# A fused encoder layer: shorter candidate lists for one group's choices, an earlier close of its gathered tiles, and pair weights on another engine

## The chip, the core and the metric

The program runs on one core of a Trainium2 chip. The metric is the device time of one execution in microseconds (us); lower is better. The core has TensorE (PE) for matmuls, VectorE (DVE), ScalarE (ACT), GpSimd (POOL) and SyncE (SP), which here only issues DMA transfers. Each engine runs its own instructions in order and meets the others at semaphores.

## What is computed

One layer of a bidirectional encoder for two groups of rows with shared weights: prompt (1024 rows) and sample (256 rows), 1024 columns, all float32. Attention comes first, then an expert retrieval, which is where most of the time goes:

```python
def layer(x):                                   # for the prompt and for the sample
    x = x + mixer(rmsnorm(x, g_mix))            # projection, windowed and dense attention, gates, output
    x = x + peer(rmsnorm(x, g_ffn))
    return rmsnorm(x, g_final)

def peer(h):                                    # 8 heads, 2 x 128 keys, 128*128 experts
    sc = einsum(h @ w_query, sub_keys)          # rows x 8 x 2 x 128
    s_top, i_top = top_k(sc, 16)
    cand = s_top[..., 0, :, None] + s_top[..., 1, None, :]      # 16 x 16 sums
    best, pos = top_k(cand, 16)                 # and the expert numbers at pos
    g = softmax(best)
    u, v = expert_u[idx], expert_v[idx]         # 128 rows of 2 x 1024 for each row of h
    return sum_k g_k * gelu(u_k . h) * v_k
```

## The kernel before

The program is a row of phases with a barrier between two of them (the helper that ends a phase has line 91): projection, attention and merge of the sample; the sample's query phase; projection, attention and merge of the prompt; and last one long mixed phase for the prompt's experts.

**The query phase of the sample** (`phase_query`). SP loads the sample's rows `xn`, the row `gffn` of the expert norm, query weights, keys, `iota`, and the row `gmix` of the prompt's first norm. VectorE waits for both norm rows (one semaphore, `gain_ld`, 32) and for ScalarE's root, scales the rows to `h_` (L1439, L1441), PE transposes them and multiplies by the query weights of one head (`qp`, L1468) and then by its keys (`sc`, L1478). `choose(h)` on VectorE finds the best 16 of 128 keys twice, for two row tiles (`top16`, L1389 to L1397), forms the 16 x 16 sums `cand` (L1410), takes the best 16 of 256, and turns each position into its two key numbers by comparing (`hit`, L1420), multiplying (L1425) and summing (L1428). Beside it GpSimd scales one tile of the prompt's rows for each head (L1327, L1329) with `gmix` and a reciprocal that VectorE makes between two heads (`invert`, L1434); PE transposes it for the projection that comes next. With the phase's end the sample's numbers and gates are stored.

**The sample's experts** are gathered beside other work: tile 0 within the prompt's projection, tile 1 within its attention and merge (class `Hidden`, named `bg` in the phases). GpSimd fetches a row of `[u | v]` per slot with an indirect DMA; VectorE makes the dot product (L165), ScalarE the gelu (L203), VectorE the weight (L174) and the sum (L182). `Plan` spreads 128 such slots over the host phase's units. At the end `load_last` (L133, L134) loads the residual and the last norm's row into memory that the phase has finished with, `finish` and `square_root` make the normed result (L188 to L195, L208), `store` (L138) writes it. In the projection, which has 80 units of one row tile and one chunk of 512 columns, all of these come after the loops; in the merge `load_last` is issued earlier and the rest comes after the last residual (L1195).

**The mixed phase** (`phase_mixed`). Five row tiles of the prompt (`GATHERED`) are computed like the sample's, by gathered rows, but the weighted sum is made on PE: for a step of two slots VectorE makes two dots (L2244), ScalarE one gelu (L2055), two weights `wgt` (L2062) and two diagonal matrices `diag` (L2069), and PE multiplies the gathered `v` rows by them into `acc` (L2387). The ring has 8 slots; GpSimd refills two when PE's matmuls on them are done (L1963). Three tiles (`DENSE`) run over all experts, by PE (L2409, L2425), with gates built as a matrix (L2232, L2372, L2044). The choices of all eight tiles are made within the phase. The class `Turns` writes one order of all this, which every engine walks for its own part; `step(n, g)` is tile n's step g, where the dots and gelu are those of pair g and weights and matmuls those of pair g − 1.

## Time and profile before

| | |
|---|---|
| median of 3 runs | 4585.46 us (4581.51 to 4603.41) |
| the profiled execution | 4589.69 us, its span 4587.9 us |
| busy | PE 3973.8, DVE 2810.5, ACT 1275.5, POOL 1256.6 us |
| moved by DMA | 1383.03 MB, 301 GB/s over the span |
| phases: sample's query | 396 to 566 us |
| prompt's projection, attention, merge | 568 to 1142, to about 1710, to 2076 us |
| mixed phase | 2076 to 4588 us |

The profile shows one execution; its times are microseconds from the start of the span. A busy share is a mean over phases with different limits. In a row of the timeline, the idle time in brackets is that of the engine before the instruction, with what ended it. A group's "idle before" adds these up over its instructions.

### The profile page before, as it was taken

To read this page: it belongs to the slowest core of one execution; us is meant where nothing else is said; L and a number is where in the kernel's file an instruction comes from. 1 tells how busy PE (TensorE), PEld (TensorE's weight loads), DVE (VectorE), ACT (ScalarE), POOL (GpSimd) and SP (SyncE) were. 2 spreads that over 40 slices of the span, in tenths; PEclk is the share of its full clock that TensorE was granted. 3 is DMA by queue.
4 is the path that set the end of the run, shared out by engine and by line. 5 is a ranking of instruction groups with operands and counts; after the bars stand their busy time and mean duration, and the time that the engine had idled before them with its cause. 6 is when DMAs were issued, how large, how long until landed. Compare 5 with 4: busy or idle time off the path is not lost.

```text
span 4587.9 us, 61700 instructions
## 1 busy us (share of the span) xinstructions
PE 3973.8 (87%) x22629; PEld 2042.4 (45%) x22629; DVE 2810.5 (61%) x6794; ACT 1275.5 (28%) x3556; POOL 1256.6 (27%) x1018
## 2 busy tenths in 40 slices
PE   7776599998799989997993677779999899999998
PEld 3454444443577764444441344433434343344443
DVE  1332856776888876663878877645555555555544
ACT  0221111221455551112233455522121221122122
POOL 0200232221534413320232232222333222332331
PEclk9888799999899999998995789889999999999999
DMA  6243398886544348756698899999999899999997
GB/s 240 76 180 120 110 364 318 335 354 233 208 176 183 143 167 341 296 227 238 260 347 325 329 396 377 357 366 374 396 411 409 347 407 369 399 402 385 391 403 300
DMA packets 353597, 1383.03 MB, mean 301 GB/s; under 512 B 27152, under 2 KB 112784, under 8 KB 233872
## 3 DMA queue, kind: packets, MB, share of 16 engines
q0 software_dynamic: 129024, 939.58, 51.5%
q1 hardware_dynamic: 162992, 395.47, 23.1%
q10 hardware_dynamic: 61280, 44.04, 2.9%
q8 instruction: 180, 2.95, 0.3%
q14 instruction: 121, 0.99, 0.1%
HBM read 1283.52 MB, written 95.47 MB: 301 GB/s over the span
## 4 chain that ended last, share of the span: by engine, by line
PE 29%; DMA 9%; DVE 9%; issue 4%; ACT 3%; POOL 1%; ACTq 0%; SPq 0%; DVEq 0%; POOLq 0%
PE prompt_exp_wk L2425 10%; PE prompt_exp_wk L2409 10%; DMA prompt_exp_ring<-in_experts_dram,prompt_exp_idx 7%; PE prompt_exp_acc L2387 5%; PE prompt_exp_wk L2333 3%; DVE prompt_exp_junk L2244 3%; DMA gates_dram<-prompt_exp_area 2%; ACT prompt_exp_diag L2069 1%; ACT prompt_exp_wgt L2062 1%; POOL prompt_exp_ring L1963 1%; DVE prompt_exp_hit L2188 1%; DVE prompt_exp_topi L2139 1%; DVE prompt_exp_hT L2232 1%; DVE prompt_exp_top L2136 0%; PE prompt_exp_wk L2372 0%
## 5 line engine op out<-in xcount | busy, mean ns | idle before, releaser
L1963 POOL DMA_INDIRECT prompt_exp_ring<-in_experts_dram,prompt_exp_idx x640 | 698.8, 1092 | 1809.3 <-PE prompt_exp_acc L2387 1605.0
L2244 DVE CUSTOM_DVE_ANT_0 prompt_exp_junk<-prompt_exp_ring,prompt_exp_h 128x1024 bf16<-128x1024 f32 x640 | 762.0, 1222 | 239.7 <-DMA prompt_exp_ring<-in_experts_dram,prompt_exp_idx 225.9
L2425 PE MATMUL prompt_exp_wk<-prompt_exp_area 128*128 128x512 f32 x1536 | 706.2, 607 | 6.5 <-DVE prompt_exp_area L2272 6.5
L2409 PE MATMUL prompt_exp_wk<-prompt_exp_hT,prompt_exp_area 128*128 128x384 f32 x2048 | 702.7, 497 | 0.0
L2387 PE MATMUL prompt_exp_acc<-prompt_exp_ring,prompt_exp_diag 32*32 32x512 f32 x10240 | 392.5, 640 | 267.8 <-ACT prompt_exp_diag L2069 267.7
L537 PE MATMUL prompt_proj_acc<-normed_w,normed_hT 128*128 128x512 f32 x1280 | 553.6, 595 | 14.5 <-PEq L91 14.5
L2409 PEld LDWEIGHTS prompt_exp_wk<-prompt_exp_hT,prompt_exp_area 128*128 128x128 f32 x2048 | 387.3, 193 | 343.9 <-issue 111.0
L152 POOL DMA_INDIRECT sample_hid_ring<-in_experts_dram,sample_hid_idx x256 | 278.8, 1089 | 893.8 <-DVE sample_hid_acc L182 844.3
L2425 PEld LDWEIGHTS prompt_exp_wk<-prompt_exp_area 128*128 128x128 f32 x1536 | 282.2, 191 | 432.7 <-issue 385.8
L2282 DVE TENSOR_TENSOR prompt_exp_area<-prompt_exp_area,prompt_exp_wk 128x512 f32<-128x512 f32 x186 | 127.7, 687 | 519.0 <-PE prompt_exp_wk L2425 495.5
L2055 ACT ACTIVATE prompt_exp_ge<-prompt_exp_dot 128x2 f32<-128x2 f32 x320 | 65.0, 203 | 1241.6 <-DVE prompt_exp_dot L2244 1240.2
L537 PEld LDWEIGHTS prompt_proj_acc<-normed_w,normed_hT 128*128 128x128 f32 x1280 | 243.6, 191 | 318.3 <-issue 318.3
L165 DVE CUSTOM_DVE_ANT_0 sample_hid_junk<-sample_hid_ring,sample_hid_h 128x1024 bf16<-128x1024 f32 x256 | 349.6, 1365 | 42.0 <-DMA sample_hid_ring<-in_experts_dram,sample_hid_idx 31.4
L182 DVE SCALAR_TENSOR_TENSOR sample_hid_acc<-sample_hid_ring,sample_hid_w,sample_hid_acc 128x1024 f32<-128x1024 f32 x254 | 330.5, 1301 | 7.4
L2387 PEld LDWEIGHTS prompt_exp_acc<-prompt_exp_ring,prompt_exp_diag 32*32 32x32 f32 x10240 | 79.4, 105 | 467.1 <-ACT prompt_exp_diag L2069 382.1
L2069 ACT ACTIVATE prompt_exp_diag<-prompt_exp_fold,prompt_exp_wgt 128x32 f32<-128x32 f32 x640 | 170.7, 314 | 10.6 <-PE prompt_exp_acc L2387 0.2
L2372 PE MATMUL prompt_exp_wk<-prompt_exp_area,prompt_exp_hT 128*128 128x128 f32 x768 | 114.8, 308 | 41.6 <-DVE prompt_exp_hT L2232 28.2
L2062 ACT ACTIVATE prompt_exp_wgt<-prompt_exp_ge,prompt_exp_g 128x1 f32<-128x1 f32 x640 | 149.0, 280 | 0.0
L537 PE MATMUL sample_proj_acc<-sample_proj_w,sample_proj_hT 128*128 128x512 f32 x320 | 139.5, 598 | 9.3 <-PEq L271 9.3
L2232 DVE TENSOR_SCALAR prompt_exp_hT<-prompt_exp_iota,prompt_exp_ijgT 128x128 f32<-128x128 f32 x384 | 106.0, 352 | 65.8 <-PE prompt_exp_wk L2372 62.6
L2372 PEld LDWEIGHTS prompt_exp_wk<-prompt_exp_area,prompt_exp_hT 128*128 128x128 f32 x768 | 106.8, 219 | 82.4 <-DVE prompt_exp_hT L2232 56.1
L998 PE MATMUL prompt_att_Op<-prompt_att_vB,prompt_att_pT_b 128*128 128x128 f32 x1024 | 125.9, 276 | 10.4 <-ACT prompt_att_pT_a L712 10.4
(363 smaller groups left out, 4987.8 us busy)
## 6 DMA issues: line engine op xcount, KB each, us to landing
prompt_exp_area<-in_u_turned_dram SPq DMA_DIRECT2D x128, 512.0 KB, 8.4
prompt_exp_area<-in_experts_dram SPq DMA_DIRECT2D x64, 1024.0 KB, 13.3
gates_dram<-prompt_exp_area ACTq DMA_DIRECT2D x12, 2048.0 KB, 29.2
prompt_exp_area<-gates_dram SPq DMA_DIRECT2D x32, 768.0 KB, 14.6
sample_proj_w<-in_w_all_dram SPq DMA_DIRECT2D x10, 2048.0 KB, 13.9
normed_w<-in_w_all_dram SPq DMA_DIRECT2D x10, 2048.0 KB, 15.2
proj_dram<-prompt_proj_stage SPq DMA_DIRECT2D x80, 256.0 KB, 5.4
prompt_exp_ring<-in_experts_dram,prompt_exp_idx POOLq DMA_INDIRECT x640, 10.1
```

The lines of the kernel that those rows point to most:

```text
L152: self.nc.gpsimd.indirect_dma_start(out=self.ring[:, s % self.RING, :], out_offset=None, in_=self.experts, in_offset=bass.IndirectOffsetOn ...
L165: self.nc.vector.tensor_tensor_reduce(out=self.junk[:], in0=self.ring[:, s % self.RING, 0:D], in1=self.h[:], scale=1.0, scalar=0.0, op0=AL ...
L182: nc.vector.scalar_tensor_tensor(self.acc[:], v, w, self.acc[:], ALU.mult, ALU.add).then_inc(self.added, 1)
L537: last = nc.tensor.matmul(acc[:, u % 4, :], hT[:, k, t * P:(t + 1) * P], w[:, c % NL, k, :], start=(k == 0), stop=(k == KD - 1))
L1963: nc.gpsimd.indirect_dma_start(out=ring[:, s % RING, :], out_offset=None, in_=experts, in_offset=bass.IndirectOffsetOnAxis(ap=idx[:, n % 2 ...
L2062: last = nc.scalar.activation(wgt[:, s:s + 1], ge[:, s:s + 1], ACT.Copy, scale=g2[:, n % 2, s:s + 1])
L2069: last = nc.scalar.activation(diag[:, (g - 1) % 2, c, :], fold[:], ACT.Copy, scale=wgt[:, s:s + 1])
L2244: nc.vector.tensor_tensor_reduce(out=junk[:, s % 2, :], in0=ring[:, s % RING, 0:D], in1=h2[:, n % 2, :], scale=1.0, scalar=0.0, op0=ALU.mu ...
L2372: last = nc.tensor.matmul(wk[:, 2 + i % 2, c * KEYS:(c + 1) * KEYS], onehot_a[:, i % 2 * BLOCK + c, :], onehot_b[:, i % 2, c, :], start=Tr ...
L2387: last = nc.tensor.matmul(acc[at:at + Q, part, :], diag[k, (g - 1) % 2, c, :], ring[k, s % RING, D + half * 512:D + half * 512 + 512], sta ...
L2409: last = nc.tensor.matmul(wk[:, j % 2, 0:TURNED], ut[:, j % 3, k, :], hT_dense[:, k, :], start=(k == 0), stop=(k == KD - 1))
L2425: last = nc.tensor.matmul(wk[:, 2 + o % 2, :], act_e[:, c % 2, j, t * P:(t + 1) * P], vt[:, half, j, :], start=(j == 0), stop=(j == JB - 1))
```

## The change

1. In `phase_query`, `choose(h)` forms 80 of the 256 sums for each row tile: all 16 with the best first key, 7 x 8 for the next seven, and 8 with the best second key (only these can be among the best 16). The position in this list is turned into two key numbers by five small operations on float32 and compared, in bf16, with two rows of a `table`. Comparing takes two instructions of 512 elements, multiplying one of 1024.
2. `gmix` gets a semaphore of its own, `mix_ld`, which GpSimd waits for; VectorE waits for `gffn` alone.
3. In `phase_project`, the plan of the gathered tile ends at unit 77 (`UNITS - 3`). SP issues `load_last` at unit 74; `square_root` and `finish` are made at unit 77. The tile's store stays at the end.
4. In `phase_merge`, `finish` is made ahead of the last residual.
5. In the mixed phase the pair's two weights are one product on VectorE, at the start of `step(n, g)`, after a wait for the gelu of pair g − 1. ScalarE's two activations and the semaphore `gates_ready` go.

```diff
 # phase_project
-        plan = Plan(0, SLOTS, UNITS, 1, 1)
+        plan = Plan(0, SLOTS, UNITS - 3, 1, 1)
...
+                    if bg and u == UNITS - nt + 2:
+                        sp.wait_ge(mm_tile, nt * (CHUNKS - 1))
+                        bg.load_last(sp, w[:, (CHUNKS - 2) % NL, :, :].rearrange("p (a k) c -> p a (k c)", k=KD // 4))
...
                 if bg:
-                    sp.wait_ge(mm_tile, nt * (CHUNKS - 1))
-                    bg.load_last(sp, w[:, (CHUNKS - 2) % NL, :, :].rearrange("p (a k) c -> p a (k c)", k=KD // 4))
                     bg.store(sp)
...
+                    if bg and u == UNITS - 3:
+                        bg.square_root(act)
...
+                    if bg and u == UNITS - 3:
+                        bg.finish(dve)
 # phase_merge
+                    if bg and i + 1 == G:
+                        bg.finish(dve)
                     dve.wait_ge(x_ld, 16 * (i + 1))
                     dve.wait_ge(z_full, i + 1)
                     nc.vector.tensor_tensor(xt[:], Z[:], xt[:], ALU.add).then_inc(res_ready, 1)
 # phase_query
-                sp.dma_start(gmix[:], g_mix.broadcast_to([P, D])).then_inc(gain_ld, 16)
+                sp.dma_start(gmix[:], g_mix.broadcast_to([P, D])).then_inc(mix_ld, 16)
...
-                pool.wait_ge(gain_ld, 32)
+                pool.wait_ge(mix_ld, 16)
...
+                        nc.vector.tensor_tensor(cand[:, i, ROW:ROW + 56].rearrange("p (a b) -> p a b", b=HALF_ROWS),
+                                                top[:, i, 0, 1:HALF_ROWS].unsqueeze(2).to_broadcast(block),
+                                                top[:, i, 1, 0:HALF_ROWS].unsqueeze(1).to_broadcast(block), ALU.add)
+                    nc.vector.tensor_tensor(cand[:, :, 0:ROW], top[:, :, 0, 0:1].to_broadcast([P, B, ROW]), top[:, :, 1, :], ALU.add)
...
+                    top16([(best[:, i, h, :], pos[:, 0, i, :], cand[:, i, :], crest[:, i, :]) for i in each])
...
+                    for p in range(2):
+                        last = nc.vector.tensor_tensor(hit[:, :, p, :, :], ab[:, p, :, :].unsqueeze(3).to_broadcast(square),
+                                                       table[:, p:p + 1, :].unsqueeze(1).to_broadcast(square), ALU.is_equal)
...
-                dve.wait_ge(gain_ld, 32)
+                dve.wait_ge(gain_ld, 16)
 # phase_mixed, ScalarE
-                        act.wait_ge(gelued, STEPS * n + g)
-                        for s in range(pair.start, pair.stop):
-                            last = nc.scalar.activation(wgt[:, s:s + 1], ge[:, s:s + 1], ACT.Copy, scale=g2[:, n % 2, s:s + 1])
-                        last.then_inc(weighted, 1)
                         act.wait_ge(weighted, STEPS * n + g)
 # phase_mixed, VectorE
                 def step(n, g):
+                    if g >= 1:
+                        dve.wait_ge(gelued, STEPS * n + g)
+                        c = slice(PAIR * (g - 1), PAIR * g)
+                        nc.vector.tensor_tensor(wgt[:, c], ge[:, c], g2[:, n % 2, c], ALU.mult).then_inc(weighted, 1)
```

How the instructions stand, at three places. VectorE in the query phase, the end of one head's choice, before:

```order
L1415 TENSOR_SCALAR sample_qry_posd<-sample_qry_pos 128x2x16
L1416 TENSOR_SCALAR sample_qry_posd<-sample_qry_pos 128x2x16
L1417 CAST sample_qry_posf<-sample_qry_posd 128x64
L1420 TENSOR_TENSOR sample_qry_hit<-sample_qry_posf,sample_qry_iota 128x256 x4
L1425 TENSOR_TENSOR sample_qry_hit<-sample_qry_hit,sample_qry_topf 128x256 x4
L1428 TENSOR_REDUCE sample_qry_sel<-sample_qry_hit 128x64
```

and changed:

```order
L1421 TENSOR_SCALAR sample_qry_pos<-sample_qry_pos 128x32
L1422 CAST sample_qry_posf<-sample_qry_pos 128x64
L1424 TENSOR_SCALAR sample_qry_part<-sample_qry_posf 128x32
L1425 SCALAR_TENSOR_TENSOR sample_qry_part<-sample_qry_posf 128x32
L1426 TENSOR_TENSOR sample_qry_ab<-sample_qry_part,sample_qry_posf 128x32
L1427 SCALAR_TENSOR_TENSOR sample_qry_part<-sample_qry_posf,sample_qry_part 128x32
L1428 SCALAR_TENSOR_TENSOR sample_qry_ab<-sample_qry_posf,sample_qry_part 128x32
L1431 TENSOR_TENSOR sample_qry_hit<-sample_qry_ab,sample_qry_table 128x2x256 x2
L1434 TENSOR_TENSOR sample_qry_hit<-sample_qry_hit,sample_qry_topb 128x1024
L1437 TENSOR_REDUCE sample_qry_sel<-sample_qry_hit 128x64
```

Three small operations have become seven, and the eight operations on `hit` three; the sum over `hit` stands as it did.

SP at the end of the prompt's projection, before (L410 are the units' stores, L425, L427 and L430 those of the keys):

```order
L410 DMA proj_dram<-prompt_proj_stage 128x512 x5
L425 DMA prompt_kta_dram<-prompt_proj_kT 512x1x128
L427 DMA prompt_ktb_dram<-prompt_proj_kT 256x1x128
L410 DMA proj_dram<-prompt_proj_stage 128x512 x5
L430 DMA prompt_rb_dram<-prompt_proj_rB 128x80
L133 DMA normed_w<-x_dram 128x1024
L134 DMA normed_w<-in_g_final_dram 128x1024
L138 DMA out_dram<-normed_w 128x1024
L395 UNCONDITIONAL_BRANCH
```

and changed (L428, L430 and L433 are the same stores):

```order
L410 DMA proj_dram<-prompt_proj_stage 128x512 x5
L133 DMA normed_w<-x_dram 128x1024
L134 DMA normed_w<-in_g_final_dram 128x1024
L428 DMA prompt_kta_dram<-prompt_proj_kT 512x1x128
L430 DMA prompt_ktb_dram<-prompt_proj_kT 256x1x128
L410 DMA proj_dram<-prompt_proj_stage 128x512 x5
L433 DMA prompt_rb_dram<-prompt_proj_rB 128x80
L138 DMA out_dram<-normed_w 128x1024
L395 UNCONDITIONAL_BRANCH
```

The two loads of L133 and L134 stand ahead of the last key stores and the stores of the last five units, and only L138 is left behind the last.

The mixed phase, ScalarE at its first steps, before:

```order
L2055 ACTIVATE prompt_exp_ge<-prompt_exp_dot 128x2
L2062 ACTIVATE prompt_exp_wgt<-prompt_exp_ge,prompt_exp_g 128x1 x2
L2069 ACTIVATE prompt_exp_diag<-prompt_exp_fold,prompt_exp_wgt 128x32 x2
L2055 ACTIVATE prompt_exp_ge<-prompt_exp_dot 128x2
L2062 ACTIVATE prompt_exp_wgt<-prompt_exp_ge,prompt_exp_g 128x1 x2
L2069 ACTIVATE prompt_exp_diag<-prompt_exp_fold,prompt_exp_wgt 128x32 x2
```

and changed:

```order
L2060 ACTIVATE prompt_exp_ge<-prompt_exp_dot 128x2
L2067 ACTIVATE prompt_exp_diag<-prompt_exp_fold,prompt_exp_wgt 128x32 x2
L2060 ACTIVATE prompt_exp_ge<-prompt_exp_dot 128x2
L2067 ACTIVATE prompt_exp_diag<-prompt_exp_fold,prompt_exp_wgt 128x32 x2
L1996 COPY prompt_exp_area<-prompt_exp_wk 128x512
```

VectorE at the same steps of the first tile, before:

```order
L2139 MAX_INDEX prompt_exp_pos<-prompt_exp_best,prompt_exp_rest 128x8
L2244 ISA prompt_exp_junk,prompt_exp_dot<-prompt_exp_ring,prompt_exp_h 128x1024
L2244 ISA prompt_exp_dot 128x1
L2244 ISA prompt_exp_junk,prompt_exp_dot<-prompt_exp_ring,prompt_exp_h 128x1024
L2244 ISA prompt_exp_dot 128x1
L2244 ISA prompt_exp_junk,prompt_exp_dot<-prompt_exp_ring,prompt_exp_h 128x1024
L2244 ISA prompt_exp_dot 128x1
L2244 ISA prompt_exp_junk,prompt_exp_dot<-prompt_exp_ring,prompt_exp_h 128x1024
L2244 ISA prompt_exp_dot 128x1
```

and changed (L2242 are the dots):

```order
L2137 MAX_INDEX prompt_exp_pos<-prompt_exp_best,prompt_exp_rest 128x8
L2234 TENSOR_TENSOR prompt_exp_wgt<-prompt_exp_ge,prompt_exp_g 128x2
L2242 ISA prompt_exp_junk,prompt_exp_dot<-prompt_exp_ring,prompt_exp_h 128x1024
L2242 ISA prompt_exp_dot 128x1
L2242 ISA prompt_exp_junk,prompt_exp_dot<-prompt_exp_ring,prompt_exp_h 128x1024
L2242 ISA prompt_exp_dot 128x1
L2234 TENSOR_TENSOR prompt_exp_wgt<-prompt_exp_ge,prompt_exp_g 128x2
L2242 ISA prompt_exp_junk,prompt_exp_dot<-prompt_exp_ring,prompt_exp_h 128x1024
L2242 ISA prompt_exp_dot 128x1
L2242 ISA prompt_exp_junk,prompt_exp_dot<-prompt_exp_ring,prompt_exp_h 128x1024
L2242 ISA prompt_exp_dot 128x1
```

ScalarE has lost the row of two weights of each step, and VectorE has one product ahead of each pair of dots, of the pair before it.

## Rows read from the trace of the kernel before

**Rows 1.** The page, part 1: busy us (share of the span) xinstructions.

```profile
PE 3973.8 (87%) x22629; PEld 2042.4 (45%) x22629; DVE 2810.5 (61%) x6794; ACT 1275.5 (28%) x3556; POOL 1256.6 (27%) x1018
```

**Rows 2.** Timeline, query phase: start us, us, engine, line, tiles [idle <-releaser].

```profile
401.94 8.01 SPq L1298 DMA_DIRECT2D sample_qry_gmix<-in_g_mix_dram  x1
...
404.77 0.29 ACT L1364 ACTIVATE sample_qry_stat<-sample_qry_stat,sample_qry_eps 128x2 f32<-128x2 f32 x1
410.00 1.14 SPq L1288 DMA_DIRECT2D sample_qry_xt<-in_x_dram  x2
419.92 0.17 DVE L1439 RECIPROCAL sample_qry_stat<-sample_qry_stat 128x2 f32<-128x2 f32 x1 [23.32 <-DMA sample_qry_gmix<-in_g_mix_dram]
...
437.37 0.17 DVE L1434 RECIPROCAL sample_qry_stat<-sample_qry_stat 128x1 f32<-128x1 f32 x1 [14.76 <-ACT sample_qry_stat L1347]
...
452.92 0.17 DVE L1434 RECIPROCAL sample_qry_stat<-sample_qry_stat 128x1 f32<-128x1 f32 x1
```

**Rows 3.** DMA issues of 385:600: KB each, median us from issue to landing.

```profile
sample_qry_gffn<-in_g_ffn_dram SPq DMA_DIRECT2D x1, 512.0 KB, 7.4
```

**Rows 4.** Timeline of the end of the prompt projection and the next start.

```profile
1126.87 0.45 SPq L133 DMA_DIRECT2D normed_w<-x_dram  x1
...
1131.58 1.22 DVE L188 TENSOR_TENSOR normed_w<-sample_hid_acc,normed_w 128x1024 f32<-128x1024 f32 x1 [3.96 <-DMA normed_w<-in_g_final_dram]
...
1137.28 0.34 SPq L138 DMA_DIRECT2D out_dram<-normed_w  x1
1142.14 0.32 SPq L719 DMA_DIRECT2D prompt_att_q<-proj_dram  x1
```

**Rows 5.** Timeline of the end of the prompt merge.

```profile
2063.86 1.22 DVE L1195 TENSOR_TENSOR prompt_mrg_xt<-prompt_mrg_Z,prompt_mrg_xt 128x1024 f32<-128x1024 f32 x1 [6.90 <-PE prompt_mrg_Z L1235]
...
2070.70 0.34 SPq L138 DMA_DIRECT2D out_dram<-prompt_mrg_mixT  x1
```

**Rows 6.** Windows, mixed phase: us, busy us by engine, PEclk, DMA share, GB/s.

```profile
2300.00:2600.00 300.00, 191.20 (x1818) 89.65 (x1817) 246.43 (x868) 109.21 (x347) 89.87 (x84) 0.77 0.86 334
2600.00:3040.00 440.00, 319.41 (x2838) 187.24 (x2836) 294.80 (x888) 211.19 (x631) 120.27 (x106) 0.90 0.98 371
3040.00:4570.00 1530.00, 1445.80 (x9872) 620.08 (x9856) 820.56 (x1752) 311.50 (x1188) 455.77 (x418) 0.99 0.98 387
```

**Rows 7.** The chain of waits, pieces of L2062: the first and last of 88.

```profile
2290.02 0.47 ACT prompt_exp_wgt L2062 x2
...
4556.59 0.47 ACT prompt_exp_wgt L2062 x2
```

**Rows 8.** VectorE by form, 436:566: xcount | busy us, mean ns | idle.

```profile
L1420 DVE TENSOR_TENSOR sample_qry_hit<-sample_qry_posf,sample_qry_iota 128x256 f32<-128x256 f32 x32 | 11.5, 420 | 0.3
...
L1389 DVE MAX8 sample_qry_best<-sample_qry_cand 128x8 f32<-128x256 f32 x16 | 6.0, 418 | 0.3
```

**Rows 9.** VectorE's groups by form, 2600:4560 (mixed phase).

```profile
L2188 DVE TENSOR_TENSOR prompt_exp_hit<-prompt_exp_ab,prompt_exp_table 128x1024 bf16<-128x1024 bf16 x16 | 19.6, 1225 | 0.5
...
L2136 DVE MAX8 prompt_exp_best<-prompt_exp_rest 128x8 f32<-128x80 f32 x64 | 15.7, 245 | 2.2
...
L2190 DVE TENSOR_TENSOR prompt_exp_hit<-prompt_exp_hit,prompt_exp_topb 128x1024 bf16<-128x1024 bf16 x16 | 11.1, 692 | 0.6
...
L2177 DVE SCALAR_TENSOR_TENSOR prompt_exp_part<-prompt_exp_posf,prompt_exp_part 128x64 f32<-128x64 f32 x8 | 1.8, 219 | 0.0
```

**Rows 10.** Timeline of the query phase, one of PE's queries.

```profile
523.90 6.37 PE L1468 MATMUL sample_qry_qp<-sample_qry_hT,sample_qry_wq 128*128 128x256 f32 x25
```

**Rows 11.** VectorE's groups by form, 583:2060 (sample's tiles), the products.

```profile
L174 DVE TENSOR_TENSOR sample_hid_w<-sample_hid_ge,sample_hid_g 128x1 f32<-128x1 f32 x192 | 47.8, 249 | 117.5 <-ACT sample_hid_ge L203 117.3
...
L174 DVE TENSOR_TENSOR sample_hid_w<-sample_hid_ge,sample_hid_g 128x4 f32<-128x4 f32 x16 | 14.3, 893 | 0.0
```

**Rows 12.** The page, part 5: xcount | busy, mean ns | idle before, releaser.

```profile
L2387 PE MATMUL prompt_exp_acc<-prompt_exp_ring,prompt_exp_diag 32*32 32x512 f32 x10240 | 392.5, 640 | 267.8 <-ACT prompt_exp_diag L2069 267.7
...
L2055 ACT ACTIVATE prompt_exp_ge<-prompt_exp_dot 128x2 f32<-128x2 f32 x320 | 65.0, 203 | 1241.6 <-DVE prompt_exp_dot L2244 1240.2
```

More of the change, by code:

```diff
@@ L518, in _ @@
                         dve.wait_ge(kr_ready, k + 1)
-                if bg:
-                    bg.finish(dve)
             if bg:
@@ new lines, in choose @@
+                    link(nc.vector.tensor_copy(posf[:], pos[:]))
+                    at, row = posf[:, 0, :, :], posf[:, 1, :, :]
+                    nc.vector.tensor_scalar(part[:, 0, :, :], at, 63.0, 1.0, ALU.subtract, ALU.max)
+                    link(nc.vector.scalar_tensor_tensor(part[:, 1, :, :], row, 2.0, row, ALU.is_ge, ALU.mult))
+                    nc.vector.tensor_tensor(ab[:, 0, :, :], part[:, 0, :, :], row, ALU.max)
+                    link(nc.vector.scalar_tensor_tensor(part[:, 1, :, :], at, 1.0 / HALF_ROWS, part[:, 1, :, :], ALU.mult, ALU.subtract))
@@ L1780, in phase_mixed @@
         Turns(lambda what, *a: order.append(a[:2]) if what == "choose" and a[2] == 0 else None).walk()
-        gate_order = []
-        Turns(lambda what, *a: gate_order.extend([a] if what == "gates" and a[0] in GATHERED else [])).walk()
-        def gates_upto(tile, h):
-            return 1 + next(i for i, (t, hs) in enumerate(gate_order) if t == tile and hs.start <= h < hs.stop)
         def walk(**do):
@@ L2066, in step @@
                             act.wait_ge(used, STEPS * n + g - 2)
-                        for s in range(pair.start, pair.stop):
-                            c = s % PAIR
+                        for c in range(PAIR):
+                            s = PAIR * (g - 1) + c
                             last = nc.scalar.activation(diag[:, (g - 1) % 2, c, :], fold[:], ACT.Copy, scale=wgt[:, s:s + 1])
@@ L2204, in gates @@
                     to = gd_of(tile - DENSE[0]) if tile in DENSE else g2[:, tile % 2, :]
-                    if tile in GATHERED and tile >= 2 and hs.start == 0:
-                        dve.wait_ge(diag_ready, STEPS * (tile - 1))
                     dve.wait_ge(exp_ready, gated)
@@ L2211, in gates @@
                                                  ssum[:, hs].unsqueeze(2).to_broadcast([P, hs.stop - hs.start, TOPK]), ALU.mult))
-                    if tile in GATHERED:
-                        dve.sem_inc(gates_ready, 1)
                 def turn(d):
```

51 lines of the change are left out of this document (20 added, 31 removed).

## The prediction

> **What bounds the kernel now.** I read the page first, then the waits and the chain around each edited place. PE is busy for 87% of the span and DVE for 61% [rows 1], but that is a mean over ten phases with a barrier between them, so every edit has to be priced in its own phase, by what ends last there.
>
> *Query phase (396 to 566 us).* VectorE sits idle for 23.32 us and then runs the reciprocal from which everything follows, at 419.92; the wait that ended last is the norm row gmix, which doesn't even enter that work. ScalarE's square root was there at 404.77 + 0.29 = 405.06 [rows 2], and gffn, the row that VectorE really multiplies by, landed 7.4 us after its issue, while gmix was issued behind it at 401.94 [rows 2, 3]. From 437.37 on VectorE works through eight heads. One takes 15.55 us (437.37 to 452.92), the next begins with no idle before it, so the choosing itself bounds this stretch [rows 2].
>
> *Projection tail.* The loads of the residual and of the last norm's row are issued only after the last unit, at 1126.87; then come a VectorE wait of 3.96 us for them, sum, squares, root, scaling, a store at 1137.28, and the next phase at 1142.14 [rows 4]. *Merge tail:* the loads come early there, but the same arithmetic stands behind the residual of 2063.86; its store goes out at 2070.70 [rows 5].
>
> *Mixed phase (2076 to the end, over half of the span).* A step goes from VectorE (two dots) to ScalarE (gelu, two weights, two diagonals), to TensorE (32 matmuls) and to the ring slot that GpSimd refills. From 3040 on, DMA shows a share of 0.98 and PE is busy for 1445.80 of 1530 us; in 2600:3040 PE is busy for only 319.41 of 440, in 2300:2600 for 191.20 of 300, while VectorE shows 246.43 there [rows 6]. The chain of waits passes through ScalarE's pair of weights at 88 places, most of them 0.47 us long, together 38.4 us [rows 7].
>
> **The change, part by part.** The sum is made against the profiled execution, 4589.69 us, which lies 4.2 above the median of 4585.46; the gains then come off the median.
>
> 1. *Norm row on its own semaphore.* VectorE waits for gffn and the root alone and can start at 405.1. Scaling, transposes, copies, the first query and its scores took 17.4 us, from 419.92 to the reciprocal of the first choice at 437.37. From 405.1 that gives 422.5. A second input appears here: that reciprocal needs the squares of xt, which SP issues at 410.00, behind the 8.01 us of gmix's own issue [rows 2]; landing, squares and root bring it to about 423. The later one counts: 437.4 − 423 = **14.5**. If wq or the keys, on the same full queues, come a little later, less: I take 10 to 15.
>
> 2. *Lists of 80.* Per head ten searches (MAX8, FIND_INDEX8, MATCH_REPLACE8) run over 256 sums. MAX8 takes 418 ns over 256 and 245 over 80 [rows 8, 9]; the other two are priced alike: 10 × 0.173 = 1.73. Forming the sums stays even: two operations become four short ones. Decoding has four operations more, 219 ns each in the mixed phase: −0.88. The hits: eight operations of 420 become two compares of 512 elements (half of 1225 and a fixed part, 0.65) and one bf16 multiplication, 692 [rows 8, 9]: 3.36 − 1.99 = 1.37. Less 0.1 for bubbles this is 2.12 per head, times eight **17.0**, a period of 13.4. Next would be PE and GpSimd: after the reciprocal GpSimd scales for some 5.3 us, then PE has transposes, scores and a query of 7.88 [rows 10] that end about 16.6 after it; the next round wants PE at 13.4 + 5.3 = 18.7. Two us of cover remain; if they go, part of the 17 does. Range 10 to 20.
>
> A page of the Trainium skill bears on this: by "VectorE: DVE Perf Modes", section "What auto-detection actually checks", operations on 16-bit tensors with step ±1 run at double rate. The multiplication agrees (692 for 1024 elements), the compare, one input of which repeats along its last dimension, does not (1225 for as many). Were both compares at double rate, they would gain 8 × 0.5 = 4 us more.
>
> 3. *Tile closed within the projection.* SP issues the two loads five units before the end, ahead of the last stores of the keys; those don't wait for them, they only share the queue. The arithmetic follows unit 77 of 80. Behind the last unit stays the tile's store, which can go out at 1126.87, where the loads stood, instead of 1137.28: **10.4** [rows 4]. The next phase follows a store by 4.86 us as before. The arithmetic on VectorE (some 6 us with its wait for ScalarE's root) lies inside a unit of 6.87 us in which VectorE has no copy to make that PE needs sooner; if it were in the way, PE would wait for a few us. Compressing the plan to 77 units adds 0.1 item of 1.3 us to each, which the idle of VectorE takes. Range 8 to 12.
>
> 4. *Tile closed within the merge.* VectorE waits 6.90 us for PE's last output before the residual of 2063.86 [rows 5]. The same 6 us fit in with under 1 to spare. The store then goes out behind that of x, near 2066 rather than 2070.70: **4.6**, range 3 to 6.
>
> 5. *Pair weights on VectorE.* ScalarE loses 640 activations; VectorE gains 320 products of 128x2. The nearest row is the 128x1 product of the sample's tile, 249 ns on the mean over 192 [rows 11]. Some of those ran against GpSimd's arithmetic, which the mixed phase hasn't got, so I take 0.17, near the short ones. At the 88 places of the chain 0.47 becomes 0.17 plus hand-overs: 23 saved. Against it stands the new wait: VectorE may not begin step g before ScalarE's gelu of g − 1. Where two steps stand back to back, the second loses the gelu (203 ns [rows 12]), a hand-over of 0.06 and the product: 0.43. In the order of the change 69 of the 320 products stand directly behind another step's dots; if 30 of them are on the path, this is 13. Left: **10**. Bounds: all that was on the chain (38.4), and a loss of 7 if all 69 pay. Queued behind the waiting product are VectorE's choices and area sums, and PE waits for those.
>
> Sum: 14.5 + 17.0 + 10.4 + 4.6 + 10 = 56.5. Profiled 4533.2; against the median 4585.46 − 56.5 = **4529**. The 46.5 of the first four parts can't be given back later, since a barrier stands behind each of their phases.
>
> **The rivals.** (a) *The mixed phase is held by transfers.* At a DMA share of 0.98 from 3040 on [rows 6], relief on ScalarE turns into waiting for rows: term 0, 4539. Against it: PE is busy for 94% there too, and in 2300:2600 the share is only 0.86. (b) *The whole chain share is won:* 4585.5 − 46.5 − 38.4 = 4501. For it: 30 of the 88 places lie in 2600:3040, where PE is idle for over a quarter. (c) *Choosing falls back on PE's loop, or its operations cost more:* 17.0 lost, 4546. (d) *The change doesn't do what it says at the norm row*, since another late load (keys, wq) ends the wait: 14.5 lost, 4543. (e) *The products are stretched by GpSimd.* The 128x4 products of the sample's tile, which run in the attention phase beside GpSimd's multiplications, average 893 ns [rows 11]. At the 88 places 0.89 would cost 78 in place of 38.4: 4585.5 − 46.5 + 40 = 4579. Against it: GpSimd runs only row gathers in the mixed phase. The Trainium skill ("SBUF — State Buffer", section "Who interferes with whom") names the case: two SBUF inputs on VectorE contend with a GpSimd instruction that reads SBUF. (f) *Slower: VectorE is tied to ScalarE's queue.* That queue runs in order, so a gelu also waits behind copies that wait for PE. If each of the 320 steps pays the 0.43 and once more as much in area sums that reach PE late, 275 are lost: 4585.5 − 46.5 + 275 = 4814. It decides from 46.5 / 0.86 = 54 steps on, by over 0.5% from 81. Against it: after 3040 VectorE is idle for 46% of the time, where a wait costs nothing.
>
> **How the numbers follow.** Forecast 0.48, (a) 0.16, (b) 0.13, (c) 0.05, (d) 0.04, (e) 0.07, (f) 0.07. The range goes from somewhat below (b) to beyond (c) with the upper bounds of the unknown costs: 4494 to 4562; (e) and (f) are left out. 0.5%, about what a measurement of this kernel can tell from no change, is 23 us: faster by more 0.87, within it 0.08 (most of (e), the weak end of (f)), slower by more 0.05.
>
> **What would show it.** The reciprocal of sample's h near 405, choices each 13.4 us; the tile's store under 2 us behind the last unit's copy in the projection and directly behind x's in the merge; ScalarE's weights gone, VectorE's products at 0.17, some with idle before them that gelu ended; PE's idle before the expert matmuls, 267.8 now [rows 12], smaller by 10 to 25. Wrong would be a gain of the first four parts under 38, or a mixed phase whose length changed by more than 38 either way.

## The result and the profile after

The changed kernel takes 4532.68 us (median of 4 runs, 4524.0 to 4540.46) against 4588.01 us before (4 runs, 4581.51 to 4603.41). The ratio is 0.9872, with a 95% interval of 0.9855 to 0.9888: 59 us less, between 51 and 66. The profiled execution took 4540.46 us with a span of 4538.3, the longest of the four.

The page of the change, parts 1 and 5 (xcount | busy, mean ns | idle before, what ended it):

```profile
PE 3980.2 (88%) x22629; PEld 2042.2 (45%) x22629; DVE 2817.1 (62%) x7124; ACT 1126.1 (25%) x2916; POOL 1267.1 (28%) x1018
...
L2242 DVE CUSTOM_DVE_ANT_0 prompt_exp_junk<-prompt_exp_ring,prompt_exp_h 128x1024 bf16<-128x1024 f32 x640 | 765.2, 1222 | 195.6 <-DMA prompt_exp_ring<-in_experts_dram,prompt_exp_idx 195.3
...
L2385 PE MATMUL prompt_exp_acc<-prompt_exp_ring,prompt_exp_diag 32*32 32x512 f32 x10240 | 396.4, 647 | 240.8 <-ACT prompt_exp_diag L2067 238.4
```

Against [rows 1, 12]: ScalarE is busy for 149 us less, VectorE for 7 more, and PE idles for 240.8 us before the expert matmuls instead of 267.8.

The query phase in the timeline (start us, us, engine, line, tiles, idle and its end); it began 0.4 us later than in [rows 2]:

```profile
400.90 7.84 SPq L1301 DMA_DIRECT2D sample_qry_gmix<-in_g_mix_dram  x1
...
405.67 0.17 DVE L1448 RECIPROCAL sample_qry_stat<-sample_qry_stat 128x2 f32<-128x2 f32 x1 [8.69 <-ACT sample_qry_stat L1367]
...
408.79 1.15 SPq L1291 DMA_DIRECT2D sample_qry_xt<-in_x_dram  x2
...
423.63 0.16 DVE L1443 RECIPROCAL sample_qry_stat<-sample_qry_stat 128x1 f32<-128x1 f32 x1 [10.81 <-ACT sample_qry_stat L1350]
...
437.01 0.16 DVE L1443 RECIPROCAL sample_qry_stat<-sample_qry_stat 128x1 f32<-128x1 f32 x1
```

VectorE's first reciprocal now waits for ScalarE's root, not for the row gmix. The first choice begins at 423.63 instead of 437.37, and the next 13.38 us later instead of 15.55. VectorE's groups of this stretch by form:

```profile
L1431 DVE TENSOR_TENSOR sample_qry_hit<-sample_qry_ab,sample_qry_table 128x512 bf16<-128x512 bf16 x16 | 10.3, 688 | 0.3
...
L1434 DVE TENSOR_TENSOR sample_qry_hit<-sample_qry_hit,sample_qry_topb 128x1024 bf16<-128x1024 bf16 x8 | 5.5, 692 | 0.3
...
L1392 DVE MAX8 sample_qry_best<-sample_qry_cand 128x8 f32<-128x80 f32 x16 | 3.1, 235 | 0.3
...
L1427 DVE SCALAR_TENSOR_TENSOR sample_qry_part<-sample_qry_posf,sample_qry_part 128x32 f32<-128x32 f32 x8 | 1.5, 184 | 0.0
```

The end of the projection in the timeline, to be held against [rows 4]:

```profile
1059.69 0.43 SPq L133 DMA_DIRECT2D normed_w<-x_dram  x1
...
1074.76 1.23 DVE L188 TENSOR_TENSOR normed_w<-sample_hid_acc,normed_w 128x1024 f32<-128x1024 f32 x1
...
1081.74 1.28 DVE L195 SCALAR_TENSOR_TENSOR normed_w<-normed_w,sample_hid_stat 128x1024 f32<-128x1024 f32 x1
...
1093.05 0.58 ACT L447 COPY prompt_proj_stage<-prompt_proj_acc 128x512 f32<-128x512 f32 x1 [6.28 <-PE prompt_proj_acc L538]
...
1094.50 0.45 SPq L138 DMA_DIRECT2D out_dram<-normed_w  x1
1099.46 0.32 SPq L720 DMA_DIRECT2D prompt_att_q<-proj_dram  x1
```

Of the tile's work only its store is left behind the last unit's copy. From the start of that copy to the next phase it takes 6.41 us; before, from 1125.42 to 1142.14, 16.72. The end of the merge, against [rows 5]:

```profile
2013.09 1.23 DVE L188 TENSOR_TENSOR prompt_mrg_mixT<-sample_hid_acc,prompt_mrg_mixT 128x1024 f32<-128x1024 f32 x1 [0.87 <-DMA prompt_mrg_mixT<-in_g_final_dram]
...
2017.49 1.28 DVE L195 SCALAR_TENSOR_TENSOR prompt_mrg_mixT<-prompt_mrg_mixT,sample_hid_stat 128x1024 f32<-128x1024 f32 x1
...
2019.13 1.23 DVE L1198 TENSOR_TENSOR prompt_mrg_xt<-prompt_mrg_Z,prompt_mrg_xt 128x1024 f32<-128x1024 f32 x1 [0.36 <-PE prompt_mrg_Z L1236]
2020.38 0.32 SPq L1111 DMA_DIRECT2D x_dram<-prompt_mrg_xt  x1
2020.74 0.43 SPq L138 DMA_DIRECT2D out_dram<-prompt_mrg_mixT  x1
2027.12 0.32 SPq L1933 DMA_DIRECT2D prompt_exp_ring<-x_dram  x1
```

From the start of the residual to the next phase it is 7.99 us instead of 12.29. The normed tile is ready 0.36 us before PE's last output: the arithmetic just fits, the more narrowly as it first waits 0.87 us for its loads.

The mixed phase starts at 2027.12 instead of 2076.15, 49.03 earlier. Its length in the two profiled executions is 2511.2 us, and 2511.7 before, so this pair shows no gain there. Its windows, moved by the same 49 us as the phase, answer to [rows 6] (busy us by engine, then PEclk, DMA share, GB/s):

```profile
2251.00:2551.00 300.00, 191.88 (x1800) 89.07 (x1814) 248.25 (x891) 88.42 (x260) 91.05 (x84) 0.76 0.86 333
2551.00:2991.00 440.00, 328.59 (x2838) 192.05 (x2806) 297.26 (x952) 186.78 (x524) 125.00 (x106) 0.89 0.96 363
2991.00:4521.00 1530.00, 1451.13 (x9895) 621.39 (x9898) 849.34 (x1974) 213.57 (x770) 461.71 (x418) 0.98 0.98 389
```

In the second window, in which the gates of the dense tiles are built (the build stage), PE is busy 9 us longer (328.59 for 319.41), but for the same 2838 matmuls and at a granted clock of 0.89 instead of 0.90: it is no more work done. In the last window the granted clock is 0.98 instead of 0.99, and the mean expert matmul, 640 ns in [rows 12], is 647 here. The pair therefore says little of 10 us in 2500, and more runs had to. The waits of the mixed phase (us in total, times, longest):

```profile
PE prompt_exp_acc L2385 <- ACT prompt_exp_diag L2067: 238.4, 125, 20.2
...
DVE prompt_exp_junk L2242 <- DMA prompt_exp_ring<-in_experts_dram,prompt_exp_idx: 195.3, 126, 6.1
...
DVE prompt_exp_wgt L2234 <- ACT prompt_exp_ge L2060: 76.4, 77, 9.3
...
ACT prompt_exp_area L2049 <- DMA gates_dram<-prompt_exp_area: 50.3, 4, 16.2
...
PE prompt_exp_wk L2370 <- DVE prompt_exp_hT L2226: 45.1, 20, 12.2
```

The new wait is in the third row: VectorE, ahead of its product, waits 76.4 us for the gelu. Its wait for gathered rows is 30 us shorter than before (225.9). Others wait longer: PE 45.1 us for the one-hot operands of the dense tiles, which VectorE makes (28.2 before), and ScalarE 50.3 for stores of the gates (27.2 before).

### The profile page after: what moved, and what is told of

Its sections match the earlier page's. It is cut to its first block, busy times and chain, and to the rows that moved or that the text cites. A ratio compares the mean times of both kernels' runs of the same rounds, so it can differ in the third digit from the quotient of the medians.

```text
span 4538.3 us, 61378 instructions
## 1 busy us (share of the span) xinstructions
PE 3980.2 (88%) x22629; PEld 2042.2 (45%) x22629; DVE 2817.1 (62%) x7124; ACT 1126.1 (25%) x2916; POOL 1267.1 (28%) x1018
## 4 chain that ended last, share of the span: by engine, by line
PE 29%; DMA 11%; DVE 9%; issue 3%; ACT 2%; POOL 1%; ACTq 1%; SPq 0%; DVEq 0%; POOLq 0%
PE prompt_exp_wk L2407 10%; PE prompt_exp_wk L2423 9%; DMA prompt_exp_ring<-in_experts_dram,prompt_exp_idx 7%; PE prompt_exp_acc L2385 5%; DMA gates_dram<-prompt_exp_area 4%; DVE prompt_exp_junk L2242 4%; PE prompt_exp_wk L2331 4%; ACT prompt_exp_diag L2067 1%; DVE prompt_exp_hit L2186 1%; POOL prompt_exp_ring L1968 1%; DVE prompt_exp_topi L2137 1%; DVE prompt_exp_hT L2226 1%; ACTq L2100 1%; PE prompt_exp_wk L2345 0%; DVE prompt_exp_hit L2188 0%
## 5 line engine op out<-in xcount | busy, mean ns | idle before, releaser
L1968 POOL DMA_INDIRECT prompt_exp_ring<-in_experts_dram,prompt_exp_idx x640 | 710.6, 1110 | 1793.6 <-PE prompt_exp_acc L2385 1589.8
L2242 DVE CUSTOM_DVE_ANT_0 prompt_exp_junk<-prompt_exp_ring,prompt_exp_h 128x1024 bf16<-128x1024 f32 x640 | 765.2, 1222 | 195.6 <-DMA prompt_exp_ring<-in_experts_dram,prompt_exp_idx 195.3
L2385 PE MATMUL prompt_exp_acc<-prompt_exp_ring,prompt_exp_diag 32*32 32x512 f32 x10240 | 396.4, 647 | 240.8 <-ACT prompt_exp_diag L2067 238.4
L2370 PE MATMUL prompt_exp_wk<-prompt_exp_area,prompt_exp_hT 128*128 128x128 f32 x768 | 116.6, 312 | 52.0 <-DVE prompt_exp_hT L2226 45.1
L999 PE MATMUL prompt_att_Op<-prompt_att_vB,prompt_att_pT_b 128*128 128x128 f32 x1024 | 125.9, 276 | 10.4 <-ACT prompt_att_pT_a L713 10.4
L203 ACT ACTIVATE sample_hid_ge<-sample_hid_dot 128x1 f32<-128x1 f32 (+1 forms) x208 | 39.4, 203 | 349.4 <-DVE sample_hid_dot L165 349.2
```

The lines of the kernel that those rows point to most:

```text
L1968: nc.gpsimd.indirect_dma_start(out=ring[:, s % RING, :], out_offset=None, in_=experts, in_offset=bass.IndirectOffsetOnAxis(ap=idx[:, n % 2 ...
L2242: nc.vector.tensor_tensor_reduce(out=junk[:, s % 2, :], in0=ring[:, s % RING, 0:D], in1=h2[:, n % 2, :], scale=1.0, scalar=0.0, op0=ALU.mu ...
L2370: last = nc.tensor.matmul(wk[:, 2 + i % 2, c * KEYS:(c + 1) * KEYS], onehot_a[:, i % 2 * BLOCK + c, :], onehot_b[:, i % 2, c, :], start=Tr ...
L2385: last = nc.tensor.matmul(acc[at:at + Q, part, :], diag[k, (g - 1) % 2, c, :], ring[k, s % RING, D + half * 512:D + half * 512 + 512], sta ...
```

## The experiments

The kernel before ran beside each set, so each ratio is to the runs of before on the same chip; 1% is 46 us.

**1 and 2. The fifth part alone, and all but it.** The first is the kernel before with this and no other part, the second the change without it:

```diff
+                    if g >= 1:
+                        dve.wait_ge(gelued, STEPS * n + g)
+                        c = slice(PAIR * (g - 1), PAIR * g)
+                        nc.vector.tensor_tensor(wgt[:, c], ge[:, c], g2[:, n % 2, c], ALU.mult).then_inc(weighted, 1)
```

> The kernel before with the fifth part alone: the pair weights as one product on VectorE. Theory 1 (the forecast's step): relief on ScalarE's chain less VectorE's new waits, about 10 us faster than before, between 38 faster and 7 slower. Theory 2 (transfers hold the mixed phase): within 3 us of before. The two profiles of before and of the change have mixed phases of 2511.8 and 2511.2 us, which speaks for theory 2.

> The change without its fifth part: norm row, short lists, both early closes. Both theories: 46.5 us faster than before by the forecast's sum; 49 by the difference of the two profiles at the start of the mixed phase. By theory 1 it is then some 10 slower than the whole change, by theory 2 within 3 of it.

Alone: 4577.37 us (7 runs) for 4591.98, ratio 0.9967 (0.9953 to 0.9980), 15 us less. All but it: 4547.69 (5 runs), ratio 0.9898 (0.9881 to 0.9915), 47 less. 15 and 47 make 62, against 59 for the whole. Theory 2, that transfers hold the phase and the part is worth at most 3 us, falls: a gain of 9 us is the least that the interval leaves.

**3. The product behind the dots.**

```diff
-                    if g >= 1:
-                        dve.wait_ge(gelued, STEPS * n + g)
...
                             nc.vector.tensor_tensor_reduce(
...
+                    if g >= 1:
+                        dve.wait_ge(gelued, STEPS * n + g)
```

> The whole change, but VectorE makes the product of pair g - 1 behind the dots of pair g and not ahead of them. ScalarE's diagonals of pair g - 1 wait for the dots of pair g anyway (the gelu of g stands ahead of them), so nothing becomes later, and VectorE no longer waits for a gelu just begun. Theory 1 with the stalls on the path (76.4 us of idle over 77 waits in the profile of the change): 10 to 15 us faster than the change. Theory 2: the idle goes from VectorE's rows all the same, and the time stays within 3 us.

4527.73 us (5 runs), ratio 0.9854 (0.9836 to 0.9873). That is 5 us under the change by the medians and 8 by the ratios, with intervals that overlap, so the gain is likely and not settled. Its waits:

```profile
PE prompt_exp_acc L2385 <- ACT prompt_exp_diag L2067: 228.6, 127, 20.5
DVE prompt_exp_junk L2238 <- DMA prompt_exp_ring<-in_experts_dram,prompt_exp_idx: 224.9, 137, 7.0
...
DVE prompt_exp_wgt L2244 <- ACT prompt_exp_ge L2060: 29.5, 11, 7.4
```

Of the 76.4 us of waiting for the gelu 29.5 are left, and 29.6 have come back as waiting for gathered rows: of the 46.9 that went, more than half only changed their name. The stalls were not worth the 10 to 15 that the expectation gave them, nor clearly more than the 3 of theory 2.

**4. No weights at all.** The diagonals are made with `scale=ge[:, s:s + 1]`, and VectorE's product is left out, so the sum lacks its gates. It is a bound, not a kernel to use.

> The whole change without any weights in the mixed phase: the diagonals are made from the gelu directly, so the softmax gates are left out of the sum there. It is the bound of what taking work from this chain can give. Theory 1: 15 to 30 us faster than the change (88 places of 0.17 and a hand-over, and no stalls). Theory 2: under 5 us faster.

4515.56 us (5 runs), ratio 0.9832 (0.9814 to 0.9851): 17 us under the change by the medians, 18 by the ratios, within the 15 to 30 of theory 1. With this order of ScalarE's queue, leaving the weights out altogether takes some 32 us from the phase (run 4 against run 2; 30 by the ratios); moving them got about half of that.

**5. The norm row alone.** The four lines on `mix_ld` and `gain_ld`.

> The kernel before with the norm row's own semaphore alone. Forecast's step 1: VectorE's first reciprocal goes from 419.9 to about 405, the first choice from 437.4 to 423, the time down by 14.5. Rival (another late load ends the wait): the first choice moves by under 5. The profile of the change has it at 423.6 with a query phase that began 0.4 later, so this run should show 13.5 to 14.5.

4579.96 us (10 runs), ratio 0.9966 (0.9952 to 0.9981), 16 us less. The timeline:

```profile
405.27 0.17 DVE L1439 RECIPROCAL sample_qry_stat<-sample_qry_stat 128x2 f32<-128x2 f32 x1 [8.60 <-ACT sample_qry_stat L1364]
...
420.66 0.59 ACT L1358 COPY sample_qry_qT<-sample_qry_qp 128x512 f32<-128x512 f32 x1 [9.06 <-PE sample_qry_qp L1468]
421.22 1.06 ACT L1343 ACTIVATE sample_qry_sqj<-sample_qry_xt 128x1024 bf16<-128x1024 f32 x1
...
422.81 0.17 DVE L1434 RECIPROCAL sample_qry_stat<-sample_qry_stat 128x1 f32<-128x1 f32 x1 [14.85 <-ACT sample_qry_stat L1347]
...
438.35 0.16 DVE L1434 RECIPROCAL sample_qry_stat<-sample_qry_stat 128x1 f32<-128x1 f32 x1
```

The first choice starts 14.6 us earlier (437.37 before), the mixed phase at 2061.5, 14.7 earlier. The reciprocal of that choice still waits for ScalarE's root over xt: from 405.27 on, 17.54 us pass instead of the 17.45 of before. But xt is not what is late. ScalarE waits 9.06 us for PE's queries, copies them, and squares xt 0.56 us after the start of that copy, where 0.48 us passed before. So xt's load, which SP issues at 408.79, delayed the choice by 0.1 us at most.

**6. The lists alone.**

> The kernel before with the lists of 80 in the sample's choices alone; both norm rows still on one semaphore. Forecast's step 2: a head takes 13.4 us instead of 15.5, 17 us in all. Rival (the choices fall back on the loop of PE and GpSimd): a period of 14 or more, with idle of VectorE before the reciprocal of each head. The first choice should still begin near 437.

4569.18 us (10 runs), ratio 0.9960 (0.9948 to 0.9972), 18 us less. All eight reciprocals between the choices, in the view of their tile (duration min/median/max, first and last start):

```profile
L1442 DVE RECIPROCAL sample_qry_stat<-sample_qry_stat x8: 164/164/164, 436.7 to 530.0; 128x1 f32<-128x1 f32 x8
```

(530.0 − 436.7) / 7 = 13.33 us for a head; before, (545.8 − 437.4) / 7 = 15.49. Only the first of the eight has idle before it (14.4 us, ended by ScalarE's root). The rival, that the choices fall back on the loop of PE and GpSimd, falls.

**7. Both early closes alone.**

> The kernel before with both early closes alone (projection and merge). Forecast's steps 3 and 4: 10.4 and 4.6, together 15. By the profile of the change: 11.6 for the projection, of which 1.3 before its last unit, and 6.3 from the start of the attention to the mixed phase, of which 4.3 behind the last residual. If what came ahead of the tails belongs to the closes, this run shows it; if it is scatter between executions, this run shows about 14.6 in the tails alone.

4575.48 us (10 runs), ratio 0.9968 (0.9955 to 0.9981), 15 us less. The timeline at the end of the projection and of the merge:

```profile
1126.53 0.59 ACT L447 COPY prompt_proj_stage<-prompt_proj_acc 128x512 f32<-128x512 f32 x1 [6.28 <-PE prompt_proj_acc L538]
...
1127.98 0.45 SPq L138 DMA_DIRECT2D out_dram<-normed_w  x1
1132.91 0.32 SPq L720 DMA_DIRECT2D prompt_att_q<-proj_dram  x1
```

```profile
2054.64 1.23 DVE L1198 TENSOR_TENSOR prompt_mrg_xt<-prompt_mrg_Z,prompt_mrg_xt 128x1024 f32<-128x1024 f32 x1 [0.28 <-PE prompt_mrg_Z L1236]
2055.89 0.32 SPq L1111 DMA_DIRECT2D x_dram<-prompt_mrg_xt  x1
2056.26 0.43 SPq L138 DMA_DIRECT2D out_dram<-prompt_mrg_mixT  x1
2062.65 0.32 SPq L1929 DMA_DIRECT2D prompt_exp_ring<-x_dram  x1
```

6.38 us from the last copy to the next phase (16.72 before, so 10.3 less), and 8.0 from the residual (12.29 before, 4.3 less). The stretches ahead of the tails are not shorter here, so the 1.3 and 2 us that the change's profile showed there do not come from the closes. The four parts one by one gave 16, 18 and 15 us (runs 5 to 7), 49 in all, against 47 together (run 2).

**8. Diagonals ahead of the next gelu.** In the change ScalarE's queue has, for a step g, the gelu of pair g and then the diagonals of pair g − 1. Those had thereby to wait for dots with which they have nothing to do.

```diff
-                    if g < STEPS:
-                        act.wait_ge(dotted, SLOTS * n + PAIR * (g + 1))
-                        c = slice(PAIR * g, PAIR * (g + 1))
-                        nc.scalar.activation(ge[:, c], dot[:, c], ACT.Gelu).then_inc(gelued, 1)
                     if g >= 1:
                         act.wait_ge(weighted, STEPS * n + g)
...
                         last.then_inc(diag_ready, 1)
+                    if g < STEPS:
+                        act.wait_ge(dotted, SLOTS * n + PAIR * (g + 1))
+                        c = slice(PAIR * g, PAIR * (g + 1))
+                        nc.scalar.activation(ge[:, c], dot[:, c], ACT.Gelu).then_inc(gelued, 1)
```

> The whole change, but ScalarE makes the diagonals of pair g - 1 ahead of the gelu of pair g, so they no longer wait for the dots of pair g and PE can have them up to 2.4 us sooner at a step that VectorE has just begun. Theory 1 (the latency of the chain dots, gelu, weights, diagonals to PE bounds a part of the mixed phase): PE's idle before the expert matmuls (238 us) falls, and the time by 10 us or more against the change. Theory 3 (VectorE's wait for the gelu is what is left): no gain, since each gelu now stands behind two diagonals that wait for PE, and the wait of the product for the gelu (76 us) grows.

4491.38 us (5 runs, 4490.05 to 4497.84), ratio 0.9787 (0.9771 to 0.9802): 41 us under the change by the medians and 39 by the ratios, four times what was asked for. Its waits:

```profile
DVE prompt_exp_junk L2242 <- DMA prompt_exp_ring<-in_experts_dram,prompt_exp_idx: 234.1, 152, 5.9
...
PE prompt_exp_acc L2385 <- ACT prompt_exp_diag L2063: 154.7, 55, 18.9
...
DVE prompt_exp_wgt L2234 <- ACT prompt_exp_ge L2068: 75.7, 75, 10.5
```

PE's wait for the diagonals fell from 238.4 us in 125 times to 154.7 in 55. VectorE's wait for the gelu did not grow. Theory 1 holds: the way from a pair's dots to PE is what part of this phase waits for.

**9. The same order, with the weights on ScalarE.** The second kernel, with the turn of the eighth: two weights, two diagonals, then the gelu.

> The change with its fifth part undone (weights back on ScalarE) and ScalarE's order turned: weights and diagonals of pair g - 1 ahead of the gelu of pair g. It parts the move of the weights from the order of ScalarE's queue. Theory 4 (the order alone is worth some 40 us, and the engine of the weights the same 15 as without it): about 4505, 15 slower than the change with early diagonals and 25 or more faster than the change. Theory 5 (early diagonals pay only where ScalarE is relieved of the weights): 4530 or more.

4481.99 us (5 runs, 4472.91 to 4490.63), ratio 0.9760 (0.9736 to 0.9785), the fastest of all, 51 us under the change by the medians. Both theories missed: with the early diagonals the weights on ScalarE are no longer dearer by 15 us. By the medians this kernel is 9 us faster than the eighth, by the ratios 12, but the intervals overlap a little, so that it is faster is likely and not settled. Its waits:

```profile
DVE prompt_exp_junk L2255 <- DMA prompt_exp_ring<-in_experts_dram,prompt_exp_idx: 287.3, 172, 7.2
...
PE prompt_exp_acc L2398 <- ACT prompt_exp_diag L2076: 169.6, 64, 21.2
```

PE still waits 169.6 us for the diagonals, 15 more than in the eighth run, and yet the time isn't longer. VectorE has no product (nor a wait for a gelu), and idles for rows instead, 287.3 us. On ScalarE the weights of pair g − 1 can now be made while VectorE works on the dots of g, which would put their 0.48 us beside other work.

Where a product on VectorE costs time can be read from the starts of the 320 gelus in each timeline, in us from the start of the mixed phase (one profiled execution each):

| | 60th gelu | 80th | 120th | 320th |
|---|---|---|---|---|
| before | 555.9 | 698.0 | 1036.0 | 2484.3 |
| 2, all but the fifth part | 558.2 | 700.2 | 1035.4 | 2481.4 |
| 1, the fifth part alone | 558.4 | 707.2 | 1046.4 | 2476.6 |
| the change | 556.8 | 712.0 | 1048.9 | 2484.3 |
| 3, product behind the dots | 552.2 | 696.8 | 1029.3 | 2461.2 |
| 8, early diagonals | 549.2 | 706.3 | 1034.7 | 2434.9 |
| 9, the same, weights on ScalarE | 544.0 | 694.1 | 1027.5 | 2425.6 |

Between the 60th and the 80th gelu, in the build stage, the product ahead of the dots costs 7 to 13 us against the same order of ScalarE's queue without it (run 1 and the change against before and run 2, run 8 against run 9); behind the dots it costs under 3 (run 3). The fifth part thus loses 10 to 14 us by the 120th gelu and wins 11 to 18 behind it. Runs 8 and 9 are 12 us apart at the 80th gelu and 9 at the last.

**10. The product between the two dots**, with early diagonals.

> Early diagonals as in the eighth run, with VectorE's product between the two dots of a step, not ahead of them. VectorE's wait for the gelu (75.7 us over 75 waits in the eighth run) should fall under 35, while the diagonals come 1.2 us later. If the stalls of VectorE are worth more than that latency: 3 to 10 us faster than the eighth run. If latency is what counts: 5 or more slower.

4499.44 us (5 runs), ratio 0.9798 (0.9776 to 0.9821). VectorE waits for the gelu for 52.9 us in 16 times (the expectation had under 35), and PE for the diagonals for 184.6 (154.7 in the eighth). By the medians it is 8 us slower than the eighth and by the ratios 5, but the intervals overlap widely: it points to the latency and doesn't settle it.

**11. Diagonals on VectorE.**

```diff
+                            last = nc.vector.tensor_scalar(diag[:, (g - 1) % 2, c, :], fold[:], ge[:, s:s + 1], g2[:, n % 2, s:s + 1], ALU.mult, ALU.mult)
```

> Early diagonals, made on VectorE straight from gelu and gate as two operations of 128x32 for a step, with no weights at all and no ScalarE behind the gelu. It takes 0.53 us and two hand-overs from the chain and adds some 0.2 to VectorE for each of 320 steps (64 us busy), and VectorE must wait for PE's use of the diagonals before last. Theory 1 (latency of the chain): 5 to 20 us faster than the eighth run. Rival (VectorE's load in the build stage, and the wait for PE, cost more): equal or slower.

4505.46 us (5 runs), ratio 0.9811 (0.9788 to 0.9834), not faster than the eighth run and by the medians 14 us slower. PE's wait for the diagonals is down to 102.1 us, the least of all, but the time isn't. The view of the source line (ns min/median/max, then what VectorE waited for):

```profile
L2229 DVE TENSOR_SCALAR prompt_exp_diag<-prompt_exp_fold,prompt_exp_ge,prompt_exp_g x640: 282/298/552, 2149.9 to 4481.1; 128x32 f32<-128x32 f32 x160
...
  ACT prompt_exp_ge L2060: 86.0, 73
```

One operation takes 298 ns; a step costs VectorE about 0.5 us, not the 0.2 expected, and 86.0 us of waiting. The rival holds. The product is gone here, but its place is taken by two dearer operations.

**12. Comparisons with step 1.**

```diff
-                        last = nc.vector.tensor_tensor(hit[:, :, p, :, :], ab[:, p, :, :].unsqueeze(3).to_broadcast(square),
-                                                       table[:, p:p + 1, :].unsqueeze(1).to_broadcast(square), ALU.is_equal)
+                        last = nc.vector.tensor_tensor(hit[:, :, p, :, :], ab[:, p, :, :].unsqueeze(2).to_broadcast(square),
+                                                       full[:, p:p + 1, :, :].to_broadcast(square), ALU.is_equal)
```

> The change, with the comparisons of the sample's choices laid out so that both inputs have step 1 in the last dimension (a written-out table and the hits turned); the multiplication then has an input that repeats along its last dimension instead. By the rule of the page on the engine's modes each comparison falls from 688 to about 425 ns and the multiplication rises from 692 to about 1225; a head then takes 13.33 as before. If the rule doesn't decide here, the comparisons stay at 688.

One execution, 4543.93 us, too few to compare times by. VectorE's groups by form, for seven of the eight heads:

```profile
L1438 DVE TENSOR_REDUCE sample_qry_sel<-sample_qry_hit 128x64 f32<-128x1024 bf16 x7 | 14.0, 2001 | 0.2
L1435 DVE TENSOR_TENSOR sample_qry_hit<-sample_qry_hit,sample_qry_topb 128x1024 bf16<-128x1024 bf16 x7 | 8.6, 1225 | 0.2
...
L1432 DVE TENSOR_TENSOR sample_qry_hit<-sample_qry_ab,sample_qry_full 128x512 bf16<-128x512 bf16 x14 | 5.3, 421 | 0.2
```

The comparison takes 421 ns for 688, the multiplication 1225 for 692, both as the expectation has it by the section of the Trainium skill that the prediction names. The sum over `hit`, which now reads with a step of 16 elements, takes 2001 ns for 1220, which the expectation had left out, and the head takes 14.1 us instead of 13.4. The rule holds here, and this layout has no use for it.

## Why the prediction was right, and where not

The forecast was 4529 us, 56.5 less; measured were 4532.68, and 59 less by the ratio. For the first four parts the sizes were right, and the mechanism but for two details. For the fifth the total was right partly by luck. Point by point:

- *Norm row, 14.5.* Shown: 14.6 in the first choice (run 5). The step had xt, whose load stands behind gmix's issue, set the new start at about 423. That is not so: the way by PE's queries, priced at 17.4 us, took 17.54 from a reciprocal at 405.27 and gives 422.81 by itself, and xt took at most 0.1 of it. The two ways gave nearly the same time, so it cost nothing (and 437.4 − 423 is 14.4, not 14.5). Rival (d) fell.
- *Lists, 17.0.* Shown: 2.16 us for a head, 17.2 in all (run 6), against 2.12. The comparison took 688 ns for the 650 estimated, and MAX8 235 and the small operations 184 for the 245 and 219 taken from the mixed phase; these cancelled. Rival (c) fell: no idle before a head.
- *Projection, 10.4.* Shown: 10.3 (run 7).
- *Merge, 4.6.* Shown: 4.3 (run 7). The store goes out 5.2 us sooner behind the residual; the next phase follows it 0.9 us later than before (6.39 for 5.45), since with x's store issued 0.4 us ahead it lands 3.6 us after its issue instead of 2.6. Here the step was right in what moved. It had the store only 4.6 us sooner and the time behind it unchanged, and the two errors nearly cancel.
- *Mixed phase, 10.* Measured: 15 alone (9 to 22), and 12 as the difference of the whole and all but it. The price of the product was right (157 ns on the mean for 0.17), and rival (e), products stretched by GpSimd, fell with it: the longest of 320 took 0.24 us. On the chain of waits ScalarE's 38.4 us at 88 places became 8.2 us of products at 76 places. Both terms of the 10 were off. The saving of 23 does not follow from its own prices: 88 × (0.47 − 0.17) is 26.4, and two hand-overs of 0.06 at each place (ScalarE to VectorE and back) take 10.6 of it, which leaves 16 and a sum of 3. The stall was mis-sized too: I reckoned 30 steps of 0.43 us, 13 in all; there were 77 waits, 76.4 us in all. In 18 of them, with 53 us, ScalarE was still inside another instruction when the dots ended, mostly its copies of the gates (L2049); I had named that only as rival (f). The other 60 or so are 0.4 us each, near the 0.43, but twice as many as reckoned. Not all of this counts, as VectorE waited 30 us less for rows. What the waits cost shows in the build stage: 10 to 14 us by the 120th gelu (the table at run 9). Behind it the relief of ScalarE won 11 to 18. Rival (b) had argued from 30 places of the chain in 2600:3040 that the gain would lie there; it lies behind. Only the difference of the two terms came out near 10.
- *The signs.* PE's idle before the expert matmuls fell by 27 us, a little more than the 10 to 25 foreseen. Four parts under 38 did not come: run 2 has 47. Nor did a mixed phase changed by more than 38.

Rival (a), the transfers, was given 0.16 and is shown wrong by runs 1, 4 and 8. The last window of run 9 shows it most plainly, against the last of the change above:

```profile
2991.00:4467.00 1476.00, 1435.94 (x9848) 615.82 (x9851) 826.05 (x1754) 325.78 (x1184) 453.81 (x416) 0.99 0.99 399
```

It holds nearly the same matmuls (9848 for 9895) in 54 us less, with 399 GB/s moved instead of 389. A DMA share of 0.98 was no bound there. Rival (b), the whole chain share, did not come either; run 4 shows that with this order even no weights at all give about 32 of the 38.4.

What the prediction missed is the larger thing: it priced the weights on the path of the diagonals, but not the order in front of them. Gelu g stood ahead of diagonals g − 1 in the queue of ScalarE before and after the change, which put the two dots of a pair (2.4 us) in the path of the pair before it. Turned, this is worth 41 us with the weights on VectorE and about 66 with them on ScalarE (run 9 against run 2, by the medians; 63 by the ratios), several times the whole fifth part. And it takes away the gain of that part: in the old order moving the weights gains 12 to 15 us, in the new one it gains nothing, and probably loses 9 to 12.
